# Forgetting attention: VectorE copies each step's last group of transposed probabilities and reads the inverse sums itself

## The reference

```python
def fox_group(q, k, v, f_logit, f_bias):
    """Forgetting attention: softmax(q k^T / sqrt(d) + c_t - c_s), c = cumsum log sigmoid(f), causal."""
    ...
    def block(args):
        qi, ci, pi = args
        sc = jnp.einsum('bqhd,bkhd->bhqk', qi, k) * scale + (ci[..., :, None] - c[:, :, None, :])
        sc = jnp.where(pi[:, None] >= kpos[None, :], sc, -jnp.inf)
        p = jax.nn.softmax(sc, axis=-1)
        return jnp.einsum('bhqk,bkhd->bqhd', p, v)
```

## Time and profile before

| | us |
|---|---|
| median of 3 runs | 1349.31 (1345.33 to 1351.01) |
| the profiled execution, its own time | 1345.35 |
| its span | 1343.5 |
| the 16 steps, first to last product (L797 to L814) | about 597 to 681 |
| mean granted clock of TensorE | 0.949 of full speed |

### The profile page before, as it was taken

How to read it: one execution, slowest core, us unless ns; L and a number is a source line. 1 busy time by engine, 2 the same in 40 slices (tenths; PEclk the granted TensorE clock), 3 DMA queues, 4 the chain that set the end, 5 groups by cost and what they waited for, 6 DMA issues and landing times.

```text
span 1343.5 us, 17627 instructions
## 1 busy us (share of the span) xinstructions
PE 1187.0 (88%) x7200; PEld 659.5 (49%) x7200; DVE 505.0 (38%) x1224; ACT 395.5 (29%) x753; POOL 130.8 (10%) x126
## 2 busy tenths in 40 slices
PE   5899999999999999997899998677759999999940
PEld 4444744447545898874554444345533333333310
DVE  5322314111798256754512221256632221222118
ACT  3102631113684231136641000474201111111115
POOL 1000011110000000011000000211011111111024
PEclk9799999999999999998999999799769999999975
DMA  5311112221125433303040003410149999999536
GB/s 178 110 32 33 32 53 75 75 75 53 32 71 242 114 80 123 119 2 126 1 157 1 0 0 131 188 48 32 48 173 417 412 417 416 423 418 412 218 151 257
DMA packets 67450, 199.55 MB, mean 149 GB/s; under 512 B 25780, under 2 KB 42404, under 8 KB 56612
## 3 DMA queue, kind: packets, MB, share of 16 engines
q1 hardware_dynamic: 59328, 181.39, 35.3%
q0 software_dynamic: 7456, 16.92, 3.3%
q10 hardware_dynamic: 580, 0.05, 0.0%
HBM read 172.63 MB, written 35.14 MB: 155 GB/s over the span
## 4 chain that ended last, share of the span: by engine, by line
PE 82%; DVE 9%; ACT 3%; issue 3%; DMA 2%; ACTq 0%; POOL 0%; DVEq 0%; POOLq 0%
PE bank L2285 28%; PE bank L1414 12%; PE bank L1475 7%; PE bank L1440 6%; PE bank L750 2%; PE bank L736 2%; PE bank L1490 2%; PE bank L1530 2%; PE bank L1400 2%; PE bank L2393 2%; PE bank L811 1%; PE bank L783 1%; PE bank L2274 1%; PE bank L841 1%; DVE arena L1661 1%
## 5 line engine op out<-in xcount | busy, mean ns | idle before, releaser
L2285 PE MATMUL bank<-arena 128*128 128x512 f32 (+3 forms) x1088 | 379.4, 509 | 1.6 <-DVE arena L2090 1.6
L2285 PEld LDWEIGHTS bank<-arena 128*128 128x128 f32 x1088 | 206.5, 191 | 169.3 <-issue 154.4
L1414 PE MATMUL bank<-arena 128*32 128x512 f32 x1536 | 171.0, 597 | 2.0 <-DVE arena L1193 2.0
L1414 PEld LDWEIGHTS bank<-arena 128*32 128x32 f32 x1536 | 50.7, 111 | 117.1 <-issue 117.1
L1866 ACT ACTIVATE arena<-bank 128x512 f32<-128x512 f32 (+1 forms) x64 | 32.9, 514 | 226.3 <-PE bank L2285 226.0
L1475 PE MATMUL bank<-arena 128*128 128x512 f32 x220 | 95.6, 592 | 0.0
L1440 PE MATMUL bank<-arena 128*32 128x512 f32 x768 | 87.4, 595 | 0.7 <-ACT arena L1102 0.7
L1202 DVE TENSOR_TENSOR arena<-arena,bank 128x256 f32<-128x256 f32 x25 | 10.5, 421 | 168.8 <-ACT arena L1098 155.7
L1475 PEld LDWEIGHTS bank<-arena 128*128 128x128 f32 x220 | 41.3, 190 | 49.7 <-issue 49.7
L1854 ACT ACTIVATE arena<-arena 128x1024 f32<-128x1024 f32 x26 | 27.4, 1054 | 127.2 <-DVE arena L1262 106.2
L1262 DVE TENSOR_TENSOR arena<-arena,bank 128x512 f32<-128x512 f32 x32 | 22.0, 688 | 112.5 <-PE bank L1475 87.8
(11 more groups left out here) (372 smaller groups left out, 1634.9 us busy)
## 6 DMA issues: line engine op xcount, KB each, us to landing
arena<-in_w_e_gu SPq DMA_DIRECT2D x27, 2048.0 KB, 15.8
arena<-in_w_e_dn SPq DMA_DIRECT2D x33, 1024.0 KB
arena<-in_w_in SPq DMA_DIRECT2D x11, 1024.0 KB, 5.4
arena<-y_d SPq DMA_DIRECT2D x8, 1024.0 KB, 5.0
arena<-hz_d SPq DMA_DIRECT2D x4, 1792.0 KB, 8.1
arena<-in_w_e_gu SPq DMA_DIRECT2D x6, 1024.0 KB
arena<-in_w_e_gu SPq DMA_DIRECT2D x12, 512.0 KB
pk_d<-arena SPq DMA_DIRECT2D x8, 640.0 KB, 2.9
```

The costliest lines, as they stand in the source:

```text
L1414: ins = mm(bank[part, :], hgT[:, k, part], w_gu(es[i] % NB, k), start=(k == 0), stop=(k == KT - 1))
L2285: ins = mm(psum[PROJ_BANKS[u % 3]][0:rows, 0:n], lhs(k), rhs(k), start=(k == 0), stop=(k == KT - 1))
```

## The change

VectorE takes over two things from ScalarE. It copies the last group of each step (head 1, the last up to four blocks) in a new function `fox_rowsT`, and it copies the inverse sums itself in `fox_out`, just ahead of the multiplication (`link` puts a wait between the two). ScalarE's `sums` is gone. The last groups have a semaphore of their own, `x_pd`. A table `FOX_T` lists all groups with the engine that copies each, and TensorE waits for the right one of the two semaphores before it fills a bank again or starts the values. In VectorE's turn the order becomes biased(g), inverse(g-1), rowsT(g-1), out(g-2).

```diff
@@
+        FOX_T = []
+        for g in range(NS):
+            for par in range(2):
+                for b in range(fox_halves(g)):
+                    FOX_T.append((g, par, b, "dve" if par == 1 and b == fox_halves(g) - 1 else "act"))
+            if g == L_AT:
+                FOX_T += [(g, 2, i, "act") for i in range(CT * NHALF)]
...
+        def group_evicted(eng, j):
+
+            eng.wait_ge(s["x_pt"] if FOX_T[j][3] == "act" else s["x_pd"], by(FOX_T[j][3], j))
...
-            def sums(g):
-                act.wait_ge(s["x_pv"], g + 1)
-                if g >= 2:
-                    act.wait_ge(s["x_o"], g - 1)
-                nc.scalar.activation(x_rb[g % 2], psum[6 + g % 2][:, P:2 * P], ACT.Copy).then_inc(s["x_rs"], 1)
...
             def fox_out(g):
                 i, c = fox_step(g)
-                dve.wait_ge(s["x_rs"], g + 1)
+                dve.wait_ge(s["x_pv"], g + 1)
+                link(v.tensor_copy(x_rb[g % 2], psum[6 + g % 2][:, P:2 * P]))
                 v.tensor_tensor(x_o_[:, c, i * P:(i + 1) * P], psum[6 + g % 2][:, 0:P], x_rb[g % 2],
                                 ALU.mult).then_inc(s["x_o"], 1)
+
+            def fox_rowsT(g):
+                i, c = fox_step(g)
+                b = fox_halves(g) - 1
+                m = i + 1 - 4 * b
+                j = group_of(g, 1, b)
+                if g >= 2:
+                    dve.wait_ge(s["x_pv"], g - 1)
+                dve.wait_ge(s["x_tr"], j + 1)
+                v.tensor_copy(x_pT[g % 2][:, 1, 4 * b:4 * b + m, :],
+                              psum[4 + j % 2][:, 0:m * P].rearrange("p (b q) -> p b q", q=P)).then_inc(s["x_pd"], 1)
...
+                if g >= 1:
+                    fox_inverse(g - 1)
+                    fox_rowsT(g - 1)
                 if g >= 2:
                     fox_out(g - 2)
-                if g >= 1:
-                    fox_inverse(g - 1)
                 if g == L_AT + 2:
                     norm_dve(dve, v, link, 1, h_o, 0, a_g)
             fox_inverse(NS - 1)
+            fox_rowsT(NS - 1)
             fox_out(NS - 2)
             fox_out(NS - 1)
...
             def fox_values(g):
                 i, c = fox_step(g)
-                pe.wait_ge(s["x_pt"], fox_groups(g) + 2 * fox_halves(g))
+                if fox_halves(g) > 1:
+                    group_evicted(pe, group_of(g, 1, fox_halves(g) - 2))
+                else:
+                    group_evicted(pe, group_of(g, 0, 0))
+                group_evicted(pe, group_of(g, 1, fox_halves(g) - 1))
```

More of the change, by code:

```diff
@@ L129, in hybrid_trunk @@
             h_E h_Ee h_l1 n_sq n_ss n_rms n_gate n_out h_act l_gs x_bf x_l h_dve unit_e h_z x_row l_w l_xc x_ad
-            h_os l_act l_dve l_g h_kt h_kts x_cbp x_cb x_nb x_p x_tr x_pv x_pt x_o x_rs x_r h_o h_dS
+            h_os l_act l_dve l_g h_kt h_kts x_cbp x_cb x_nb x_p x_tr x_pv x_pt x_o x_pd x_r h_o h_dS
             h_Sv h_scr h_pm x_dg x_qk f_out t_wo t_x2 t_mq t_rw t_o_r xs_r t_xn t_m_e t_rl
@@ L318, in hybrid_trunk, with group_of @@
         L_AT = 3
+        FOX_T = []
[5 more added lines that the diff above has]
+                FOX_T += [(g, 2, i, "act") for i in range(CT * NHALF)]
+        by = lambda who, j: sum(t[3] == who for t in FOX_T[:j + 1])
+        def group_of(g, par, b):
+            return FOX_T.index((g, par, b, "dve" if par == 1 and b == fox_halves(g) - 1 else "act"))
+        def group_evicted(eng, j):
+            eng.wait_ge(s["x_pt"] if FOX_T[j][3] == "act" else s["x_pd"], by(FOX_T[j][3], j))
         l_xc = view(o_bc + CT * T, CT, T)
@@ L561, in act_tail @@
             nc.scalar.activation(n_sq[1], h_o, ACT.Square).then_inc(s["n_sq"], 1)
-            tr = [0]
             def probs(g):
@@ L571, in probs @@
                                          accum_out=x_sum[:, g, par:par + 1]).then_inc(s["x_p"], 1)
[L573 to L576, removed]
             def probsT(g):
@@ L582, in probsT @@
                 for par in range(2):
[L583 to L587, removed]
-                                             ACT.Copy).then_inc(s["x_pt"], 1)
-            def sums(g):
-                act.wait_ge(s["x_pv"], g + 1)
-                if g >= 2:
-                    act.wait_ge(s["x_o"], g - 1)
-                nc.scalar.activation(x_rb[g % 2], psum[6 + g % 2][:, P:2 * P], ACT.Copy).then_inc(s["x_rs"], 1)
+                    for b in range(fox_halves(g) - par):
+                        m = min(4, i + 1 - 4 * b)
+                        j = group_of(g, par, b)
+                        act.wait_ge(s["x_tr"], j + 1)
+                        nc.scalar.activation(x_pT[g % 2][:, par, 4 * b:4 * b + m, :],
+                                             psum[4 + j % 2][:, 0:m * P].rearrange("p (b q) -> p b q", q=P),
+                                             ACT.Copy).then_inc(s["x_pt"], 1)
             for g in range(NS):
                 probs(g)
-                if g >= 1:
-                    sums(g - 1)
                 probsT(g)
@@ L602, in act_tail @@
                     for i in range(CT * NHALF):
-                        bank = group(act)
-                        norm_ln(act, 1, i, bank).then_inc(s["x_pt"], 1)
-                    act.wait_ge(s["x_pt"], fox_groups(L_AT + 1))
+                        j = FOX_T.index((g, 2, i, "act"))
+                        act.wait_ge(s["x_tr"], j + 1)
+                        norm_ln(act, 1, i, psum[4 + j % 2]).then_inc(s["x_pt"], 1)
+                    act.wait_ge(s["x_pt"], by("act", j))
                     norm_exp(1)
-            sums(NS - 1)
             act.wait_ge(s["x_o"], NS)
@@ L784, in fox_scores, with group @@
                            b_k[rows(par), c, hf * HALF:hf * HALF + m], start=True, stop=True).then_inc(s["x_qk"], 1)
-            def group(e):
+            def group(pe):
                 if tr_pe[0] >= 2:
-                    e.wait_ge(s["x_pt"], tr_pe[0] - 1)
+                    group_evicted(pe, tr_pe[0] - 2)
             def fox_transposes(g):
```

## The result

| | before | changed kernel |
|---|---|---|
| median of 4 runs, us | 1348.61 (1345.33 to 1351.01) | 1378.08 (1375.49 to 1380.91) |
| the profiled execution's own time, us | 1345.35 | 1375.49 |
| its span, us | 1343.5 | 1373.2 |

The ratio is 1.0222, with a 95% interval of 1.0199 to 1.0245: the change makes the kernel 29.5 us slower. The profiled executions differ by 30.1 us.

A forecast was written before the change was run, and what follows sets the result against it. Turn-to-turn pace bounds it: scores(g+2) wait for biased(g+1). Direct 18.9, early 0.3 and clock 2 sum to 21.2 us, giving 1366.6 on the profiled execution, 1370.5 on the median; forecast 1368 us, 8-in-10 range 1359 to 1383.

The forecast's parts named there:

- The side and the mechanism: In turns 6 to 13, VectorE's list puts biased behind the last transposes, delaying scores every turn; slower, chance 0.92.
- The direct terms: Turns 6 to 13: lost time from transposes' end, hand-over, copies and multiplication, 1.6 to 2.8 us each, sum 18.9 us.
- turn 7: Loss of 2.5 us, its transposes taken at half clock (1.97 us); at full clock 1.6 us.
- The clock: Idle TensorE runs partly at 1.2 GHz: half of eight turns lose 0.5 us, 2 us; all eight would be 24 us.
- half clock through the stage: Rival: TensorE at 1.2 GHz in half or more lengthened turns, 3 us in each of four; 1378 us, up to 1390; chance 0.22.
- The idle stretch: TensorE in each of eight turns idles from transposes' end through rowsT, out and half of biased: 2.3 us.
- TensorE's busy time stays: Expected sign in the profile after: TensorE's share of the span falls while its busy time is unchanged.
- the excess over 20 us: Sign of being wrong: time lost beyond 20 us lies in longer matmul rows of an otherwise equal stage.
- Turns 14 to 16: No scores from turn 14; biased(15) about 3 us later but hidden; slower copy costs values 0.1 us where VectorE is free.
- The 0.3 us below turn 6: Scores there need only a turn-old biased; two short copies ahead of biased(2) may show once, 0.3 us.
- The gain from ScalarE: Sixteen inverse-sum copies and 16 group copies leave ScalarE, idle ahead of most copies; nothing credited.
- The rival in which the change does what it is aimed at: Engines copy side by side, TensorE's 6.7 us of waits for ScalarE go; 1342.6 us; needs 2.5 us slack; chance 0.03.

The follow-up runs named there:

- the stretch filled: The changed kernel with four unread 128x256 products on TensorE ahead of the scores in turns 6 to 13; 1369.92 us, ratio 1.0165 to the kernel before.
- only the sums: The kernel before with only the inverse-sums copy moved to VectorE, in its old place; ScalarE copies all groups; 1348.65 us, ratio 1.0004.
- the copy behind biased: The changed kernel with last groups of steps 6 to 15 on VectorE, copied one turn later behind biased(g+1), earlier ones on ScalarE; 1349.01 us, ratio 1.0008.
- out a turn later: The kernel before, all copies on ScalarE, with VectorE's multiplication one turn later in its list, out(g-3) for out(g-2); 1344.02 us, ratio 0.9978.
- the last copy ahead: Copies placed behind biased(g+1) as in another run, but rowsT(13) stands ahead of biased(15); 1349.0 us, ratio 1.0007 to the kernel before.
- only a wait: The kernel before, with VectorE also waiting each turn until step g-1's last group is transposed; no copy moved; 1360.05 us, ratio 1.0088.
- out first: The changed kernel with out(g-2) ahead of rowsT(g-1) in VectorE's turn; 1374.34 us, ratio 1.0204 to the kernel before.
- early stretches filled: The run with rowsT(13) ahead of biased(15), plus unread TensorE products ahead of transposes(4) and the scores of turns 6 and 7; 1352.89 us, ratio 1.0046.

## Why the prediction came out as it did

- **The side and the mechanism** were right: biased(g+1) starts behind the last transposes, in each of turns 6 to 13, and it is paid in every one. The wait alone, without any copy, made turns 6 to 13 longer by 11.2 us, and the copies behind biased by none.
- **The direct terms** were right in size. With the stretch filled, eight terms of 1.6 to 2.8 us met eight losses of 1.7 to 2.9 us, sum 18.9 against 18.9; only turn 7, where I took a slow row of transposes for its base, was 0.4 too high. That the sums agree to 0.1 us is luck in part: turn 6 was 0.2 too low, and the kernel with the stretches filled runs some rows of turns 6 and 7 at full clock that ran at half clock before. The prices of the moved copies were right to 0.01 us.
- **The clock** is the term that was mis-sized. The prediction put "half of the eight turns with 0.5 us lost each", 2 us, and gave half clock through the stage 0.22, at 1378 us. It took 10.9 us, and the time was 1378.08 us: what was measured is that rival, which is the forecast's mechanism with more half clock. Only its way there differs: the loss is spread over seven turns and is not 3 us in each of four. The idle stretch was sized right (2.3 us forecast, 2.2 to 3.0 measured). What failed is the step from there: I read the comparable stretches as "some turns in part", and turned that into 0.5 us for half of the turns without a row for it. Two more of its statements bear on this. It said that TensorE's busy time stays, and it rose by 11.7 us. And it called itself wrong if the excess over 20 us lay in longer matmul rows of an otherwise equal stage: the excess does lie there, but the stage is not otherwise equal, since the 19 us are there too.
- **Turns 14 to 16** had nothing in the sum, though the prediction named 0.1 us for the slower copy where VectorE is free. They lost 0.8 us together, 0.4 of it in values(13), which waited 1.12 instead of 0.74 us, since the values there have nothing else to wait for. The 0.3 us below turn 6 was not there: from the first product of the stage to values(4) it is 20.5 us, against 20.6 before.
- **The gain from ScalarE** was credited with nothing, and the runs agree: TensorE's 4.5 us ahead of transposes stands in every trace, because those groups stay on ScalarE in all of them. The rival in which the change does what it is aimed at needed slack in biased, and there was none: in turn 13 the transposes end 1.75 us behind the start that biased had before.
- 1368 us was 10 us too low, and the range held the time, because its upper end had 12 us for the clock. The sum, 21.2 us, was 9.2 short of the 30.4 us by which the stage grew (85.0 to 115.4, first to last product); 8.9 of that is the clock.

## What to carry to other kernels

Before a wait is moved to an engine with idle time, ask what stands behind it in that engine's list, and who waits for that. An engine that is 38% busy over the span, as VectorE is in both kernels, can still set the end through the order of its list: the copies cost 30 us ahead of the next step's work, and 26 of the 32 cost nothing behind it. And where a change makes TensorE idle in each turn of a loop, give half clock a term of its own, with the whole loop at half clock as its upper end: here the stage had 30 us more at 1.2 GHz, and it cost 11 us on top of 19, where the prediction had put 2 and reckoned 24 for all eight turns.

## What was not expected of the hardware

- Idle stretches of 1.40 us in each of turns 7 to 13 (2.3 in turn 6) left the clock at full speed in most turns, with 0.91 granted over the stage, against 0.92 in the kernel before; those of 1.7 to 2.1 us (2.7 in turn 6) gave 0.86, and those of 2.2 to 3.0 us (3.3 in turn 6) 0.81. Four unread products in the stretch brought it to 0.95 and made the kernel 8 us faster. The length of the stretch alone doesn't tell which turns are slow: in the changed kernel the scores behind 2.35 us of idleness in turn 11 kept full clock (1.13 us for four instructions), and those behind 2.21 us in turn 10 did not (3.36 us for eight).
- Identical code behind the stage took 662.0 to 662.4 us in five of the ten profiled executions (both kernels, only the sums, the copy behind biased, out a turn later), 665.1 us in one (the last copy ahead) and 666.8 to 667.7 us in four (only a wait, the stretch filled, out first, early stretches filled). The stage itself is therefore the better measure of a difference of a few us here than one execution's time. Whether an edit has a part in this is not shown.
